# The last head's retention outputs as three rounded products, with the key steps in a row ahead of the branch products

## The reference, cut to what matters

```
q, k = rotate(...), rotate(...) * RET_DK ** -0.5        # 4 retention heads, dk 128, dv 256
scores = einsum(q, k) * decay                            # decay gamma^|t-s|, both directions
ret    = scores @ v                                      # per head, 512 x 512 by 512 x 256
ret_n  = ret * rsqrt(mean(ret^2) + EPS) * ret_norm
branch_a = (silu(rg) * ret_n) @ w_ret_out
branch_b = att @ w_att_out
merged = sigmoid(g0) * branch_a + sigmoid(g1) * branch_b
x = x + merged @ w_out
```

## Time and profile before

| | us |
|---|---|
| median of 3 runs | 2398.88 (2398.83 to 2399.2) |
| the profiled execution's own time | 2399.03 |
| its span | 2397.2 |
| PE busy | 2373.5, 99% of the span |
| DVE busy | 1588.7, 66% |
| ACT busy | 1475.4, 62% |
| POOL busy | 420.3, 18% |
| mean granted clock of PE | 0.997 |

### The profile page before, as it was taken

How to read it: one execution, slowest core, us unless ns; L and a number is a source line. 1 busy time by engine, 2 the same in 40 slices (tenths; PEclk the granted TensorE clock), 3 DMA queues, 4 the chain that set the end, 5 groups by cost and what they waited for, 6 DMA issues and landing times.

```text
span 2397.2 us, 33849 instructions
## 1 busy us (share of the span) xinstructions
PE 2373.5 (99%) x11840; PEld 1983.3 (83%) x11840; DVE 1588.7 (66%) x1737; ACT 1475.4 (62%) x1705; POOL 420.3 (18%) x287
## 2 busy tenths in 40 slices
PE   8999999999999999999998999999999999999998
PEld 7888888888888888888886888888888888888886
DVE  4444454534545454445346988888888888888887
ACT  5555564533466555544234777777777777777776
POOL 1534434000053334320002000000000000000000
PEclk9999999999999999999999999999999999999999
DMA  6413321225433224122238999999999999999998
GB/s 187 127 45 99 87 74 65 71 96 203 157 93 88 82 61 126 44 83 80 87 149 315 403 392 384 376 390 377 387 390 391 386 387 382 377 387 375 402 377 314
DMA packets 213498, 557.21 MB, mean 232 GB/s; under 512 B 10944, under 2 KB 92480, under 8 KB 208320
## 3 DMA queue, kind: packets, MB, share of 16 engines
q1 hardware_dynamic: 206384, 530.76, 60.1%
q0 software_dynamic: 7056, 25.69, 3.6%
HBM read 533.34 MB, written 23.07 MB: 232 GB/s over the span
## 4 chain that ended last, share of the span: by engine, by line
PE 98%; DVE 1%; DMA 0%; issue 0%; ACT 0%; POOLq 0%; SPq 0%; DVEq 0%; ACTq 0%
PE bank L1361 43%; PE bank L1024 15%; PE bank L1069 13%; PE bank L992 8%; PE bank L1013 6%; PE bank L1044 4%; PE bank L1183 2%; PE bank L1085 2%; PE bank L1407 2%; PE bank L1164 1%; PE bank L1107 1%; PE bank L1144 1%; PE bank L1111 1%; PE bank L1150 1%; PE bank L1241 1%; PE bank L1199 0%
## 5 line engine op out<-in xcount | busy, mean ns | idle before, releaser
L2435 DVE TENSOR_TENSOR m_lo<-m_raw,m_hi 128x2048 fp32r<-128x2048 f32 x380 | 867.6, 2291 | 122.3 <-ACT m_hi L1834 118.3
L1834 ACT ACTIVATE m_hi<-m_raw 128x2048 fp32r<-128x2048 f32 x382 | 733.5, 1921 | 262.2 <-PE bank L1361 258.1
L1361 PE MATMUL bank<-m_hi,xs_hi 128*128 128x512 f32 x1032 | 321.1, 392 | 0.0
L1361 PE MATMUL bank<-m_lo,xs_hi 128*128 128x512 f32 x1032 | 318.5, 390 | 0.0
L1361 PE MATMUL bank<-m_hi,xs_lo 128*128 128x512 f32 x1032 | 318.1, 389 | 0.0
L1972 DVE TENSOR_TENSOR w_lo<-w_raw,w_hi 128x1152 fp32r<-128x1152 f32 (+4 forms) x110 | 145.4, 1347 | 187.6 <-ACT w_hi L1489 187.5
L1361 PEld LDWEIGHTS bank<-m_hi,xs_lo 128*128 128x128 f32 x1032 | 193.7, 188 | 41.1
L1361 PEld LDWEIGHTS bank<-m_lo,xs_hi 128*128 128x128 f32 x1032 | 193.7, 188 | 40.7
L1361 PEld LDWEIGHTS bank<-m_hi,xs_hi 128*128 128x128 f32 x1032 | 191.4, 188 | 38.3 <-DVE xs_lo L2457 0.2
L1024 PE MATMUL bank<-h_hi,w_hi 128*128 128x512 f32 x512 | 202.8, 396 | 0.6
L1024 PE MATMUL bank<-h_hi,w_lo 128*128 128x512 f32 x512 | 199.4, 390 | 0.0
(11 more groups left out here) (279 smaller groups left out, 4250.1 us busy)
## 6 DMA issues: line engine op xcount, KB each, us to landing
m_raw<-in_w_exp_gate SPq DMA_DIRECT2D x128, 1024.0 KB, 9.0
m_raw<-in_w_exp_up SPq DMA_DIRECT2D x128, 1024.0 KB, 7.2
m_raw<-in_w_exp_down SPq DMA_DIRECT2D x128, 1024.0 KB, 7.7
w_raw<-in_w_b SPq DMA_DIRECT2D x66, 512.0 KB, 6.0
w_raw<-in_w_a SPq DMA_DIRECT2D x24, 1024.0 KB, 5.3
w_raw<-in_w_c SPq DMA_DIRECT2D x24, 1024.0 KB, 4.7
w_raw<-in_w_d SPq DMA_DIRECT2D x8, 1024.0 KB, 6.0
xt<-in_x SPq DMA_DIRECT2D x8, 512.0 KB, 7.8
```

Of the source, the lines that this page charges most:

```text
L1361: mm = pe.matmul(ps[:, half, :], a[:, chunk + k, :], v[:, k, 512 * half:512 * (half + 1)], start=first and k == n == 0, stop=last and k == ...
L1834: act.activation(m_hi[slot.slot][:, :, :], m_raw[raw.slot][:, :, :], ACT.Copy)\
L2435: dve.tensor_tensor(m_lo[slot.slot][:, :, :], m_raw[raw.slot][:, :, :], m_hi[slot.slot][:, :, :].bitcast(F32), ALU.subtract)\
```

## The change

The last head's output step uses the three rounded products as the heads in the loop do. Its operands need the steps `h`, `l`, `v` and `w` in the first branch column. `sd_hi` has a place of its own there (`sd_hi_last`, where `rot` and `crossed` were), and the four `K` steps now follow one another, ahead of both `C 3` steps; before, `C 3 0` stood between `K 1` and `K 2`, and `C 3 1` behind `K 3`.

```diff
-                ("K", 0), ("K", 1), ("C", 3, 0), ("K", 2), ("K", 3), ("C", 3, 1),
-                ("O", 0), ("O", 1), ("O", 2), ("O", 3), ("c", 2, 0), ("A", 0), ("A", 1), ("c", 2, 1),
-                ("C", 2, 0), ("C", 2, 1)]
+                ("K", 0), ("K", 1), ("h", 0), ("K", 2), ("K", 3), ("l", 0), ("h", 1), ("v",), ("l", 1), ("w",),
+                ("C", 3, 0), ("C", 3, 1), ("O", 0), ("O", 1), ("O", 2), ("O", 3), ("c", 2, 0), ("A", 0), ("A", 1),
+                ("c", 2, 1), ("C", 2, 0), ("C", 2, 1)]
...
+        sd_hi_last, _, _ = put("sd_hi_last", [P, NT, T], F32R, at=rot_at)
...
-                    if split and i == 0:
+                    if i == 0:
                         pe.wait_ge(s_sdlo, cut.n() * 2 + 2)
                         pe.wait_ge(s_vlo, cut.n(1))
-                    if split and i == NT - 1:
+                    if i == NT - 1:
                         cut.k += 1
                     pe.wait_ge(s_out_free[outs.slot], START + outs.lap)
-                    products = ((sd_hi, v_hi), (sd_hi, v_lo), (sd_lo, v_hi)) if split else ((sd, v_r),)
+                    products = ((sd_his, v_hi), (sd_his, v_lo), (sd_lo, v_hi))
...
-                            retention_step(what, arg, False)
+                            retention_step(what, arg, sd_hi_last)
...
-                    act.activation(sd_hi[:, two, :], sd[:, two, :], ACT.Copy).then_inc(s_sdhi, 1)
+                    act.activation(sd_his[:, two, :], sd[:, two, :], ACT.Copy).then_inc(s_sdhi, 1)
...
-                    dve.tensor_tensor(sd_lo[:, two, :], sd[:, two, :], sd_hi[:, two, :].bitcast(F32),
+                    dve.tensor_tensor(sd_lo[:, two, :], sd[:, two, :], sd_his[:, two, :].bitcast(F32),
```

More of the change, by code:

```diff
@@ L328, in hybrid_encoder @@
         v_r, swish = v_g[:, 0, :, :], v_g[:, 1, :, :]
+        rot_at = cursor[0]
         rot = [put(f"rot{i}", [P, T], F32)[0] for i in range(2)]
@@ L1154, in attention_step, with retention_step @@
                                     outs.k += 1
-            def retention_step(what, arg, split):
+            def retention_step(what, arg, sd_his):
                 ret, cut = t["ret"], t["cut"]
@@ L1288, in run @@
                     elif what in "KOA":
-                        retention_step(what, arg, True)
+                        retention_step(what, arg, sd_hi)
             pe.wait_ge(s_ident, 16)
@@ L1575, in attention_step, with retention_step @@
                     outs.k += 2
-            def retention_step(what, arg):
+            def retention_step(what, arg, sd_his=sd_hi):
                 ret = t["ret"]
@@ L1792, in first_column @@
                         else:
-                            retention_step(what, arg)
+                            retention_step(what, arg, sd_hi_last)
                             if what == "A" and arg[0] == 1:
@@ L2109, in attention_step, with retention_step @@
                         outs.k += 1
-            def retention_step(what, arg, ret_head):
+            def retention_step(what, arg, ret_head, sd_his=sd_hi):
                 ret = t["ret"]
@@ L2345, in first_column @@
                         else:
-                            retention_step(what, arg, RH - 1)
+                            retention_step(what, arg, RH - 1, sd_hi_last)
                             if what == "G":
```

## The result

| | us |
|---|---|
| before, median of 20 runs | 2397.47 (2396.88 to 2399.45) |
| changed, median of 20 runs | 2402.12 (2401.43 to 2404.47) |
| changed to before | 1.0020, 95% interval 1.0014 to 1.0026 |
| predicted | 2404.8 (2401.9 to 2407.5), 5.9 us more than before |

What follows compares the result with a forecast made beforehand. PE was taken to bound the kernel, busy 2373.5 of 2397.2 us. Two columns, each 2.95 us longer (waits 4.1 less 1.16 saved), added 5.9 to 2399.03, giving 2404.9; the median 0.15 lower, 2404.8, range 2401.9 to 2407.5.

Steps and rivals of the forecast that it cites:

- DVE's line behind the Sigmoid: First branch column: DVE's subtractions, weight unit and gatings up to the norm set the column's length, 2.95 us longer.
- D: Distance from the Sigmoid's start on ACT to the transposes on PE, forecast to go from 15.89 to 18.8 us.
- The size: Each of the two branch columns was to become 2.95 us longer, 5.9 us in both.
- the subtraction: On DVE in the column: `l 0`, `l 1` and `w` were counted at 1.26 us each.
- `v_lo` loses its wait for POOL: DVE's `v_lo` in the column, beside idle POOL, was to take 1.26 us instead of the loop's 2.31.
- the rival of a slow subtraction: `v_lo` or another subtraction takes 2.31 us as in the loop: +1.05 us per group, 2406.9; chance 10%.
- PE's waits: PE waits before `K 2`, `O 0`, `O 2`, `O 3` and the transposes: 0.4, 1.5, 1.5, 0.2, 0.5 us.
- PE saves 1.16 us per column: Output products on PE: 48 rounded products replace 32 float32 records, saving 1.16 us per group, at most 2.3 in both.
- all of it is hidden: Rival: in the column only PE's arithmetic counts, 2397.4 us, or 2396.6 if `K 2` needn't wait; chance 8%.
- The clock: Rival: PE's granted clock falls in the columns, losing 1.6 to 3.2 us per group, 2408 to 2411; chance 5%.
- Nothing gives it back: Behind the transposes everything follows as before, so the 2.95 us per group stays, 5.9 us in both.
- part of it is hidden: Rival: DVE reaches the gating a microsecond sooner, so 1 to 2 us per group, 2401 to 2403; chance 16%.

## Why the prediction was right, point by point

- *DVE's line behind the Sigmoid sets the column.* Right, and shown from both sides: one subtraction more costs 1.14 us per column, one less (with a Copy less on ACT) gives 1.14 back, one Copy more on ACT costs 0.38 of its 0.95 where the clock stayed up, and with none of the work D is that of before.
- *The size.* Forecast 2.95 us per column, measured 2.53 in each. The term that was too large is the subtraction. The prediction took 1.26 from one to the next, and they took 1.14 (2.36 us for two, 454.55 to 455.69 for the third), the lower of the two bounds, three times 0.12 together, 0.37 of the 0.42 us. With 1.14 the prediction had 2.6, its own lower end. The row of the very instruction was the wrong one to go by, since it stood beside POOL too: POOL worked from 145.30 to 146.60 there, and the subtraction that began at 146.34 took 1.33 and not 1.22. The prediction saw this for the second row only. The same shape on an engine left alone was the right one. Everything else on that line, from the Sigmoid to `l 0`, over the two gatings and the weight unit, between the four output gatings and through the norm, agrees to 0.03 us.
- *`v_lo` loses its wait for POOL.* Right: 1.22 us instead of 2.31, with POOL idle in the column; the rival of a slow subtraction is out.
- *PE's waits.* Forecast 0.4, 1.5, 1.5, 0.2 and 0.5 us; by start to start 0.42, 1.24, 1.15, 0.11 and 0.37, and 0.36 more for the slower first steps behind the first four. All five are there, and the profile names the releaser forecast for four of them; for the fourth output it names none. Their sum, 3.65, less the 1.16 saved is 2.49, against 2.53.
- *PE saves 1.16 us per column, and that is the most that can be won.* The saving is right (48 products 0.12 apart), but as a bound it was too generous. The rival "all of it is hidden" was priced at 2397.4; the kernel without rounding work shows that DVE's pace and the norm leave 0.1 us of it. The 0.27 us of slack before the transposes was in the sum, but not in that bound.
- *The clock.* Right for the changed kernel, 1.00 in its columns. The argument for it, that the waits come singly and none is above 1.6, was not worth much: waits of 1.03 and 1.98, or a single one of 2.18, were enough in one column and not in the other. That the changed kernel stayed on the right side was in part luck.
- *Nothing gives it back.* Right as far as the runs can tell: the columns' 5.05 us and the 4.65 between the medians agree within the spread of the runs, and the stretch between the columns took 613.81 us for 613.72. The profiled executions do differ outside the columns, by 2 us, but so do two executions of one kernel.
- *Chances.* Slower had 0.70, by a bound of 0.2%. The difference is clear of zero, but it is 0.19%, and its interval lies on both sides of the bound, so neither "slower" nor "the same" (0.29) is settled. The time itself, 2402.12, fell where the rival "part of it is hidden" had its 2401 to 2403; that is the accident of a lower base. Its mechanism, 1 to 2 us per column, did not come: D grew by 2.53.

## What to carry to other kernels

Before work is moved from the engine that is busy 99% of the time to two that are busy 62% and 66%, look at the place: what do those two do in the microseconds before the result is needed, and how much slack has the next wait behind it? Here ACT was in a Sigmoid, DVE still had two gatings and a weight unit to do, and the slack was 0.27 us. When an operation's price is read from a trace, take the row in which the engine was alone if it will be alone, even if it is another instruction of that shape. And where such a step must stay, its parts that depend on nothing late (here `v` and `w`) belong into an earlier gap, and a wait that is removed has to be followed to the next one.

## What the runs showed of the hardware

- Behind two PE waits of 1.03 and 1.98 us with 24 products between them (1.07 and 1.97 in the other execution) the granted clock was 0.71 and 0.61 in the mean of the next 4 us: part of them ran at 1.2 GHz instead of 2.4, and there products of 256 columns stood 0.21 us apart instead of 0.12. The clock also fell behind a single wait of 2.18 us (0.71) and one of 3.30 (0.62). It did so in the second column in all four of these executions and in the first in none; with unread products in the waits it did not in one execution. In the changed kernel, with two waits of 1.0 to 1.2 us, it did not in three.
- A product's first successor behind a wait comes 0.08 to 0.1 us later than in a running row (447.90 to 448.21 where 0.23 is usual), so four waits cost another 0.36 us that no idle time shows.
- An fp32r product that follows a float32 one had a step of 0.42 instead of 0.23 us behind it; where the outputs are fp32r too it is 0.23 (463.33 to 463.56 in the changed kernel).
- A subtraction of 128x1024 with both operands in SBUF took 1.22 us on DVE while POOL did nothing. Where it started beside a POOL instruction on SBUF, it ended 1.07 to 1.08 us behind that one's end: 147.67 for 146.60 and 149.91 for 148.83. No row names an idle time for POOL: the wait shows only as a longer instruction, and by these rows an engine can be held by more than semaphores.
